# Expert units of one large expert or of four small ones, with all expert weights in one ring

## The chip, the cores and the metric

The kernel runs on one core of a Trainium2 chip. The metric is the device time of one execution in microseconds (us), the median of several. The kernel is one program: an inference step of a hybrid diffusion trunk of one layer, in 32-bit floating point throughout. The change concerns its last part, the mixture of experts.

## The reference, cut to what matters

384 tokens (128 of context, 256 latent) of width 1024 pass adaLN, three mixers and a mixture of 64 SwiGLU experts (width 256), of which each token takes 8:

```python
def moe(x, lp):                        # x: (384, 1024)
    s = sigmoid(x @ lp['w_router']); sel = s + lp['b_router']
    # the 4 best of 8 groups by their two best scores, then the 8 best experts in them
    w = take(s, eidx); w = w / sum(w) * 2.5
    hg = einsum('nd,edf->nef', x, w_gate)          # w_gate, w_up: (64, 1024, 256)
    hu = einsum('nd,edf->nef', x, w_up)
    hid = silu(hg) * hu * combine[:, :, None]
    y = einsum('nef,efd->nd', hid, w_down)         # w_down: (64, 256, 1024)
    return y + shared_expert(x)
```

Gate and up of an expert are 2.097 MB, its down matrix 1.049 MB, together 3.146 MB. How many tokens each expert gets is data. With the drawn inputs the router of the reference puts the 3072 token-expert pairs on 51 of the 64 experts. Sorted, the counts are 139, 129, 125, 124, 124, 118, 118, 116, 112, 112, 111, 110, 107, 107, 105, 103, 100, 96, 95, 87, 83, 78, 74, 70, 67 (25 experts over 64 tokens), 63, 61, 59, 48, 46, 44 (6 from 33 to 64), and 21, 21, 18, 14, 12, 11, 10, 6, 5, 4, 4, 4, 2, 2, 2, 1, 1, 1, 1, 1 (20 up to 32).

## The kernel before, in words

The core's engines each run their own program and meet at semaphores. TensorE (PE) multiplies, VectorE (DVE) and ScalarE (ACT) take its results out of PSUM, SyncE (SP) starts the weight loads, GpSimd (POOL) starts the gathers and scatters of token rows.

The routed experts are worked off in units of 128 token slots. A unit is wide or narrow. A wide unit is one expert with over 64 tokens (two units if it has over 128), a narrow one is two experts of up to 64 tokens, one in slots 0 to 63, the other in 64 to 127. Units run in a fixed rhythm of three places: wide, wide, narrow. DVE works the table of units out of the counts (stage "counts"), TensorE turns it into a row of expert numbers (stage "row") and into the table of slots (stage "table"). With the counts above there are 27 wide and 13 narrow units, 40 in all, numbered 0 to 39.

For each unit DVE makes one-hot rows (`one_hots`), TensorE multiplies them with the table (`index`), DVE takes the indices (`take_index`), POOL gathers the unit's token rows from DRAM (`gather`, only rows in use move, 4 KB each), TensorE transposes them (`transposes`, L2042) and ACT copies them out (`take_xt`). Then, in TensorE's `step(i, p)`:

- transposes of unit i+1
- `gate_up` of unit i, first half of the contraction (a wide unit: L2056, 128 columns; a narrow one: L2058 and L2059, 64 columns each, each with its own expert's weights)
- `hidden_t` of unit i-1 (L2097), `index` of unit i+4 (L1702)
- `gate_up`, second half, which ends with an increment of `gu_ready`
- `down` of unit i-1, which ends with an increment of `dn_ready`: a narrow unit in full precision (L2081, L2082), a wide one in three products of a high and a low part in the faster rounded format (L2071 to L2073). For these ACT makes the high part of the down matrix (`down_high`, L1002) in the one buffer DNH, so it waits until the previous wide unit's down is done, and DVE the low part (`down_low`, L1606).

DVE weights the result (L1630) and POOL scatters it to `y_parts` in DRAM (L1093); the last two units stay in SBUF. At the end SP loads `y_parts` back (L692) in twelve parts of 1 MB, and they are summed, added and normed.

A matmul of two 32-bit operands leaves two records in the profile, one for each of its passes.

The weights have four slots (`WSLOT`) of one expert each: one for either wide place and two for the narrow one. SP works through its list in order. It starts the loads of the first three slots at once, the fourth after the shared expert's last matmuls (`shd_ready`), since that slot holds the shared weights until then. After that the gate/up load of unit i+3 waits for `gu_ready` of unit i, the down load of unit i+2 for `dn_ready` of unit i-1. Each load is one transfer of a whole matrix:

```python
def gate_up_of(r, q):
    e = number(r)
    flat = lambda a: a[bass.ds(e, 1)].rearrange("o p n -> p (o n)")
    sp.dma_start(WSLOT[q][:, 0:2 * KD * DE], flat(w_gu)).then_inc(gu_loaded[q], 16)
```

Of the kernel before, what the change touches and what calls it, by code (L numbers as in the profile page):

```python
# [43 lines left out]
HALF = P // 2  # L44
BIG0 = NE
RTAB = P
RPAD = RTAB + 8
UNITS_MAX = NE // 2 * 3
BODY = 12
PASSES = UNITS_MAX // BODY  # L50
BR_EARLY = 7
HO_BANK = (6, 4, 5)
SH_BANK = (4, 5, 0)
WS, XGS, AHEAD, GAHEAD = 4, 3, 4, 3
# [5 lines left out]
K_ID, K_SEL, K_MASK, K_LEV, K_SCAN, K_TRI, K_ONE, K_R128, K_TOK, K_COL, K_T8, K_END, K_SUB = range(13)  # L60
K_W = [P, 2 * P, GRID_W, 7 * P, T, P, P, P, NT * 4, 2, NG * NG, 0, RTAB]
K_AT = [sum(K_W[:i]) for i in range(14)]

# [5 lines left out]
def shape_constants():  # L69
    k = np.zeros((P, K_AT[13]), np.float32)  # L70
# [19 lines left out]
    put(K_COL, np.stack([r, np.where(r < BIG0, r // 2 * 3 + 3, (r - BIG0) // 2 * 3 + r % 2 + 1)], 1))  # L90
    put(K_SUB, np.tile(np.where(r < BIG0, r % 2 * HALF - 1, -1 - P * (r - BIG0))[None].astype(np.float32), (P, 1)))
# [135 lines left out]
def trunk(nc, x, consts, cols, b_gate, w_ada, w_in, w_br, w_out, rpb, cache_k, cache_v, state, w_router, b_router,  # L227
# [5 lines left out]
    with ExitStack() as ctx:  # L233
# [106 lines left out]
        WSLOT = [bigB[:, 0:6144], bigA[:, 6144:12288], bigA[:, 0:6144], bigB[:, 13824:19968]]  # L340
        GU_W = [w[:, 0:4096].rearrange("p (g k n) -> p g k n", g=2, k=KD) for w in WSLOT]
        DN_W = [w[:, 4096:6144].rearrange("p (k n) -> p k n", k=2) for w in WSLOT]
# [3 lines left out]
        XG = [bigB[:, 19968:20992], bigB[:, 20992:22016], nT_flat[:, 0:D]]  # L346
        HID = cut(bigB, 8192, (2, DE))
# [4 lines left out]
        DNL = [cut(bigB_r, 4096, (2, D)), cut(bigA_r, 10240, (2, D))]  # L352
# [13 lines left out]
        CNT, BIG, END, STA, EON, TMP = (bigD[:, 2112 + 64 * i:2176 + 64 * i] for i in range(6))  # L366
        NSM, NBG, STS, STB, RC = (bigD[:, 1536 + 64 * i:1600 + 64 * i] for i in range(5))
        RK = cut(bigD, 1856, (NT, NE))
# [8 lines left out]
        SUBC = bigD[:, 4280:4280 + RTAB]  # L377
        RHS = cut(bigD_r, 4408, (2, 2, NT, 4))
# [5 lines left out]
        YG = ([cut(bigA, i, (2, D)) for i in (0, 2048, 6144, 8192)]  # L384
              + [cut(bigB, i, (2, D)) for i in (0, 2048, 6144, 13824, 15872, 19968)]
              + [cut(nT_flat, D, (2, D)), cut(bigD, 0, (2, D))])
# [8 lines left out]
        loaded = [sem(f"weights_loaded_{i}") for i in range(NSLOT)]  # L395
        in_small = sem("constants_loaded")
        in_cols = sem("small_vectors_loaded")
        in_x = sem("x_loaded")
        in_cache = sem("cache_then_shared_down_loaded")
        in_state = sem("state_loaded")  # L400
        in_bias = [sem("bias_loaded_then_results_written_0"), sem("bias_loaded_then_results_written_1")]
        bias_masked = sem("bias_masked")
        in_xh = sem("residual_loaded")
# [19 lines left out]
        ada_back = sem("late_ada_loaded")  # L423
# [50 lines left out]
        sh_loaded = sem("shared_weights_loaded")  # L474
        bg_loaded = sem("gate_bias_loaded")
# [31 lines left out]
        gu_loaded = [sem(f"gate_up_loaded_{i}") for i in range(WS)]  # L507
        dn_loaded = [sem(f"down_loaded_{i}") for i in range(WS)]
# [75 lines left out]


        @block.sync
        def _(sp):
# [3 lines left out]
            for n in ISSUE:  # L591
# [20 lines left out]
                elif src == "out":  # L612
                    if i == 0:
# [5 lines left out]
                        sp.dma_start(SUBC, consts[:, K_AT[K_SUB]:K_AT[K_SUB] + RTAB]).then_inc(fin_loaded, 16)  # L619
# [30 lines left out]
            def gate_up_of(r, q):  # L650
                e = number(r)
                flat = lambda a: a[bass.ds(e, 1)].rearrange("o p n -> p (o n)")
                sp.dma_start(WSLOT[q][:, 0:2 * KD * DE], flat(w_gu)).then_inc(gu_loaded[q], 16)

            def down_of(r, q):
                e = number(r)
                sp.dma_start(WSLOT[q][:, 2 * KD * DE:], wd[bass.ds(e, 1)].rearrange("o p n -> p (o n)")).then_inc(dn_loaded[q], 16)
# [6 lines left out]
            for r, q in ((BIG0, 0), (BIG0 + 1, 1), (1, 3)):  # L664
                gate_up_of(r, q)
                down_of(r, q)
# [1537 lines left out]
```

## Time and profile before

| | before |
|---|---|
| median of 3 runs | 1097.4 us (1096.2 to 1100.99) |
| the profiled execution's own time | 1096.59 us |
| its span, first to last instruction | 1094.8 us |
| TensorE busy | 1043.3 us, 95% of the span |
| mean granted TensorE clock | 0.991 of full speed |
| expert loop, first gate/up to the last one's end | 581.91 to 1038.96 us |

A row of the profile names a line of the kernel, the engine, the operation and the tiles it writes and reads. "x" is a count, "idle" the time in which the engine waited before it, with what ended that wait. A DMA share of 1.00 means that the 16 DMA engines always had packets. GB/s is what they moved.

### The profile page before, as it was taken

The numbers are of one execution on the slowest core, as the hardware profiler recorded it, in microseconds if no ns is written. First come the engines' busy times: TensorE is split into PE (matmuls) and PEld (weight loads), VectorE is DVE, ScalarE is ACT, GpSimd is POOL, SyncE is SP. The second block draws the span as 40 slices with busy tenths as digits, with TensorE's granted clock in tenths as the row PEclk, the third lists the DMA queues.
The fourth block names the chain that finished last, engine by engine and source line by source line (L and its number), as shares of the span: only waits on it lengthen the run. The fifth ranks groups of instructions, "written<-read, shape, count | busy, mean of one in ns | idle before, by whom it ended". The sixth has DMA issues, their size and how long they took to land.

```text
span 1094.8 us, 15005 instructions
## 1 busy us (share of the span) xinstructions
PE 1043.3 (95%) x4876; PEld 699.7 (64%) x4876; DVE 533.0 (49%) x1118; ACT 357.3 (33%) x481; POOL 157.0 (14%) x136
## 2 busy tenths in 40 slices
PE   4999999999899999999989999999999999999975
PEld 2599988789788897874645455555555555454532
DVE  1523544445798956945634334433344334333357
ACT  3334444327444445501423222223223222222201
POOL 0020321000000000000010323322322213221000
PEclk9999999999999999999999999999999999999998
DMA  9999775447544323740297999999999999999592
GB/s 387 413 265 395 103 98 92 156 154 258 206 173 154 151 82 98 250 151 1 97 372 272 379 407 397 421 408 396 418 419 424 401 406 421 417 410 411 224 411 104
DMA packets 54912, 306.61 MB, mean 280 GB/s; under 512 B 12550, under 2 KB 16902, under 8 KB 35920
## 3 DMA queue, kind: packets, MB, share of 16 engines
q1 hardware_dynamic: 35280, 270.63, 61.3%
q0 software_dynamic: 12256, 26.80, 10.5%
q10 hardware_dynamic: 7328, 8.55, 2.3%
q8 instruction: 29, 0.48, 0.2%
q14 instruction: 19, 0.16, 0.0%
HBM read 285.31 MB, written 36.85 MB: 294 GB/s over the span
## 4 chain that ended last, share of the span: by engine, by line
PE 58%; DMA 2%; DVE 2%; ACT 1%; issue 1%; DVEq 0%; SPq 0%
PE PS L2056 16%; PE PS L2058 8%; PE PS L2081 4%; PE PS L1945 4%; PE PS L2042 3%; PE PS L1693 3%; PE PS L2071 2%; DMA bigA<-in_w_down 2%; PE PS L2073 2%; PE PS L2072 2%; PE PS L2013 2%; PE PS L2130 1%; PE PS L1935 1%; PE PS L1933 1%; PE PS L1934 1%; PE PS L2097 1%
## 5 line engine op out<-in xcount | busy, mean ns | idle before, releaser
L1093 POOL DMA_INDIRECT y_parts<-bigB,IDX x38 | 73.9, 1944 | 327.2 <-DVE bigB L1630 318.1
L2056 PE MATMUL PS<-bigB 128*128 128x512 f32 x224 | 101.7, 597 | 0.0
L1747 PE MATMUL PS<-bigB_r 128*128 128x384 f32 x288 | 98.5, 342 | 1.3 <-ACT bigB L779 1.3
L1749 PE MATMUL PS<-bigB_r,bigA_r 128*128 128x384 f32 x288 | 96.5, 335 | 0.0
L1748 PE MATMUL PS<-nT_r,bigB_r 128*128 128x384 f32 x288 | 96.3, 334 | 0.0
L1630 DVE TENSOR_SCALAR bigB<-PS,bigD 128x1024 f32<-128x1024 f32 x40 | 51.3, 1283 | 90.2 <-PE PS L2073 55.5
L2058 PE MATMUL PS<-bigA,bigB 128*64 128x512 f32 x208 | 94.8, 598 | 0.5 <-issue 0.5
L2059 PE MATMUL PS<-bigB 128*64 128x512 f32 x208 | 94.8, 598 | 0.0
L2056 PE MATMUL PS<-bigA,bigB 128*128 128x512 f32 x208 | 94.6, 598 | 0.0
L1238 DVE TENSOR_TENSOR bigA_r<-bigA,bigB_r 128x2048 fp32r<-128x2048 f32 x18 | 41.3, 2293 | 97.6 <-ACT bigB_r L805 97.6
L1596 DVE TENSOR_TENSOR bigB<-bigB,PS 128x256 f32<-128x256 f32 x40 | 16.9, 421 | 138.1 <-ACT bigB L989 138.0
L779 ACT ACTIVATE bigB<-PS 128x384 f32<-128x384 f32 (+1 forms) x55 | 27.3, 497 | 141.5 <-PE PS L1749 70.1
L2056 PEld LDWEIGHTS PS<-bigB 128*128 128x128 f32 x224 | 40.6, 190 | 40.7 <-issue 40.7
L1761 PE MATMUL PS<-bigC_r,bigA_r 128*128 128x384 f32 x192 | 65.5, 341 | 0.0
L985 ACT ACTIVATE bigB<-PS 128x1024 f32<-128x1024 f32 x40 | 40.7, 1017 | 66.2 <-PE PS L2042 66.2
L2056 PEld LDWEIGHTS PS<-bigA,bigB 128*128 128x128 f32 x208 | 37.5, 191 | 37.3 <-issue 37.3
L989 ACT ACTIVATE bigB<-PS 128x256 f32<-128x256 f32 x40 | 15.4, 384 | 138.0 <-PE PS L2056 95.8
L1747 PEld LDWEIGHTS PS<-bigB_r 128*128 128x128 f32 x288 | 54.0, 188 | 7.6 <-issue 4.5
L2058 PEld LDWEIGHTS PS<-bigA,bigB 128*64 128x64 f32 x208 | 26.3, 136 | 46.5 <-issue 45.0
L1748 PEld LDWEIGHTS PS<-nT_r,bigB_r 128*128 128x128 f32 x288 | 54.1, 188 | 0.0
L1749 PEld LDWEIGHTS PS<-bigB_r,bigA_r 128*128 128x128 f32 x288 | 54.0, 188 | 0.0
L2071 PE MATMUL PS<-bigC_r,bigB_r 128*128 128x512 f32 x108 | 49.6, 459 | 4.1 <-DVE bigB_r L1611 4.1
(370 smaller groups left out, 2117.9 us busy)
## 6 DMA issues: line engine op xcount, KB each, us to landing
bigB<-in_w_gu SPq DMA_DIRECT2D x27, 2048.0 KB, 17.6
bigA<-in_w_gu SPq DMA_DIRECT2D x26, 2048.0 KB, 15.1
bigA<-in_w_in SPq DMA_DIRECT2D x17, 2048.0 KB, 10.0
bigB<-in_w_down SPq DMA_DIRECT2D x27, 1024.0 KB, 17.9
bigA<-in_w_down SPq DMA_DIRECT2D x26, 1024.0 KB, 18.0
bigA<-in_w_ada SPq DMA_DIRECT2D x8, 2048.0 KB, 9.0
y_parts<-bigB SPq DMA_DIRECT2D x6, 2048.0 KB, 30.1
bigB<-in_w_ada SPq DMA_DIRECT2D x3, 2048.0 KB, 20.2
```

What stands on the lines that cost most here:

```text
L1093: pool.indirect_dma_start(y_parts, bass.IndirectOffsetOnAxis(ap=IDX[:, p, 1:2], axis=0), YS[:, p % 2, :], None, bounds_check=T * TOPK - 1, ...
L1630: nc.vector.tensor_scalar(YS[:, p % 2, :].rearrange("p (a n) -> p a n", a=2), PS[:, 6:8, :], WC[:, p:p + 1], None, ALU.mult).then_inc(ys_d ...
L1747: mm(out, wh, nh, start=(k == 0), stop=False)
L1748: mm(out, wh, nl, start=False, stop=False)
L1749: last = mm(out, wl, nh, start=False, stop=(k == KD - 1))
L1761: last = mm(out, low[:, k, :], NHI2[:, k, :], start=False, stop=(k == KD - 1))
L1945: last = mm(PS[:, 6 + hf, :], G[:, k, m * P:(m + 1) * P], w[:, k, :], start=(k == 0), stop=(k == KD - 1))
L2056: last = mm(PS[:, 2 + b, :], XT[:, b, k, :], GU_W[s][:, :, k, :], start=first, stop=stop)
L2058: mm(PS[0:HALF, 2 + b, :], XT[:, b, k, 0:HALF], GU_W[2][:, :, k, :], start=first, stop=stop)
L2059: last = mm(PS[HALF:P, 2 + b, :], XT[:, b, k, HALF:P], GU_W[3][:, :, k, :], start=first, stop=stop)
L2071: mm(out, HTH[:, b, k, :], DNH[:, k, cols], start=(k == 0), stop=False)
L2081: mm(PS[0:HALF, 6 + hf, :], HT[:, b, k, 0:HALF], DN_W[2][:, k, cols], start=(k == 0), stop=(k == 1))
```

## The change

A unit is now one expert with over 32 tokens (wide), or four experts of up to 32, each in its own 32 slots and its own 32 columns of the matmul. The rhythm has six places: five wide, then one of four. With the counts above that is 33 wide units and 5 of four; the last wide one takes number 38, so there are 39 units, and place 35, the sixth one for a four, is empty: its gate/up and down are left out, its hidden transposes and index product are not.

The weights pass through one ring of 27 places of 512 KB, in the order in which TensorE uses them. A wide expert takes four places for gate/up (two contraction steps in each) and two for down. A unit of four takes sixteen places for gate/up and eight for down: a slice of each of its experts, one transfer per slice, so that it may start when the first slices are there. A rhythm of six uses 54 places, twice round the ring. `w_gu` is laid out anew on the host so that a slice is 4 KB in a row of each partition. TensorE signals after each pair of contraction steps of a four (`quad_used`), so that its places are filled again early. Semaphores of earlier stages are used again for the loads, with a base count. The table of units has other formulas and gains a diagonal matrix (DIAG), a matmul in stage "row" and three in stage "table"; a small load of constants (SUBC) goes. At the end the order of the parts changes: seven of the twelve part loads go to memory that is free by then, the other five wait for the last down.

The diff, cut to its core:

```diff
+PERIOD, BIGS = 6, 5
+RING = 27
...
+def ring_places():
+    at, n = {}, 0
+    order = []
+    for c in range(BIGS):
+        order += [("gu", c, 4), ("dn", c - 1, 2) if c else ("qdn", 0, 8)]
+    order += [("qgu", 0, 16), ("dn", BIGS - 1, 2)]
...
SyncE, start:
+            e = number(0)
+            big_gate_up(e, 0, GU_TO[0])
             sp.wait_ge(n2_out, 48)
...
+            f = number(1)
+            big_gate_up(f, 1, GU_TO[1])
+            big_down(e, 0)
+            e = number(2)
+            big_gate_up(e, 2, GU_TO[2])
+            big_down(f, 1)
+            sp.wait_ge(te_ready, 1)
+            f = number(3)
+            big_gate_up(f, 3, GU_TO[3][0:2])
+            sp.wait_ge(gu_ready, 1)
+            big_gate_up(f, 3, GU_TO[3][2:])
+            big_down(e, 2)
             sp.wait_ge(shd_ready, NT)
+            e = number(4)
+            big_gate_up(e, 4, GU_TO[4])
+            big_down(f, 3)
...
SyncE, one rhythm of six:
+                    e = number(big(0))
+                    with exists(0):
+                        sp.wait_ge(gu_ready, done + 5)
+                        big_gate_up(e, 0, GU_TO[0])
+                    with sp.If(per + 1 <= quads):
+                        experts = quad_numbers(per * -4 + (RTAB - 4))
+                        sp.wait_ge(dn_ready, done + 4)
+                        quad_down(experts, 0)
+                        sp.wait_ge(quad_used, per * 3 + 1)
+                        quad_down(experts, 1)
+                    f = number(big(1))
+                    with exists(1):
+                        sp.wait_ge(quad_used, per * 3 + 2)
+                        big_gate_up(f, 1, GU_TO[1])
+                    with exists(0):
+                        sp.wait_ge(quad_used, per * 3 + 3)
+                        big_down(e, 0)
...
+                    with sp.If(per + 2 <= quads):
+                        experts = quad_numbers(per * -4 + (RTAB - 8))
+                        sp.wait_ge(gu_ready, done + 8)
+                        quad_slices(experts, 0)
+                        sp.wait_ge(dn_ready, done + 7)
+                        quad_slices(experts, 1)
+                        sp.wait_ge(gu_ready, done + 9)
+                        quad_slices(experts, 2)
+                        sp.wait_ge(gu_ready, done + 10)
+                        quad_slices(experts, 3)
+                    with exists(4):
+                        sp.wait_ge(gu_ready, done + 10)
+                        big_down(e, 4)
...
+                    if 4 * m + c == YG_FREE:
+                        sp.wait_ge(dn_ready, units)
TensorE, gate_up:
+                    if k % 2 == 0:
+                        pe.wait_ge(quad_loaded[k // 2], ...)
+                    for h in range(4):
+                        rows = slice(h * FEW, (h + 1) * FEW)
+                        last = mm(PS[rows, 2 + b, :], XT[:, b, k, rows], PIECE[RING_AT["qgu", 0][4 * (k // 2) + h]][:, half],
+                                  start=first, stop=stop)
+                    if k in (1, 3, 5):
+                        last.then_inc(quad_used, 1)
TensorE, down of a four:
+                    for k in range(2):
+                        pe.wait_ge(quad_loaded[4 + k], ...)
+                        for hf in range(2):
+                            for h in range(4):
+                                last = mm(PS[rows, 6 + hf, :], HT[:, b, k, rows],
+                                          PIECE[RING_AT["qdn", 0][4 * k + h]][:, hf * 512:(hf + 1) * 512], ...)
TensorE, stages row and table:
+                    mm(PS[0:1, 1, 2 * RTAB:3 * RTAB], RC[:, 1:2], ident, start=True, stop=True).then_inc(pr_ready, 1)
...
+                        mm(PS[:, 3, m * P:(m + 1) * P], ones, DIAG, start=False, stop=True)
```

## Rows read from the trace of the kernel before

**Rows 1.** The page: DMA busy tenths in 40 slices of the span

```profile
DMA  9999775447544323740297999999999999999592
```

**Rows 2.** The chain that ended last: start, us, what (loop's start and end)

```profile
588.88 0.89 PE PS L2042 x8
...
599.99 0.89 PE PS L2042 x8
...
611.66 0.89 PE PS L2042 x8
612.55 3.44 PE PS L2056 x8
616.44 3.54 PE PS L2056 x8
619.99 0.57 PE PS L2081
...
623.57 1.09 PE PS L2042 x8
...
634.87 0.89 PE PS L2042 x8
...
1038.96 0.57 PE PS L2081
```

**Rows 3.** Stretches: us, busy of each engine, granted clock, DMA share, GB/s

```profile
10.00:30.00 20.00, 15.88 (x92) 8.20 (x96) 5.43 (x20) 7.59 (x16) 0.00 (x0) 1.00 1.02 433
397.40:401.40 4.00, 4.00 (x25) 4.00 (x24) 1.47 (x4) 3.93 (x4) 0.00 (x0) 1.00 1.02 417
549.00:610.00 61.00, 55.64 (x209) 29.81 (x210) 23.63 (x57) 15.84 (x22) 10.87 (x8) 1.00 0.84 333
610.00:1019.00 409.00, 408.31 (x1666) 214.05 (x1665) 154.04 (x339) 104.58 (x128) 107.03 (x69) 1.00 1.00 410
669.60:704.50 34.90, 34.90 (x145) 18.25 (x144) 13.29 (x29) 9.01 (x11) 9.82 (x6) 1.00 0.99 402
809.10:844.00 34.90, 34.90 (x144) 18.24 (x144) 13.29 (x29) 9.01 (x11) 9.81 (x6) 1.00 1.01 421
```

**Rows 4.** DMA issues: tiles, count, KB each, median us to landing

```profile
bigB<-in_w_gu SPq DMA_DIRECT2D x27, 2048.0 KB, 17.6
bigA<-in_w_gu SPq DMA_DIRECT2D x26, 2048.0 KB, 15.1
...
out_y<-bigB SPq DMA_DIRECT2D x3, 512.0 KB, 2.6
```

**Rows 5.** The down loads' line (L657), 600 to 670 us

```profile
DMA to landing us min/median/max: 8.4/13.2/16.0
```

**Rows 6.** The same line, 950 to 1010 us

```profile
DMA to landing us min/median/max: 22.9/24.2/27.1
```

**Rows 7.** Timeline, 32-column matmuls of the conditioning vector's projection

```profile
37.40 1.92 PE L1731 MATMUL PS<-bigD,csil 128*32 128x512 f32 x16
37.86 0.13 PEld L1731 LDWEIGHTS PS<-bigD,csil 128*32 128x32 f32 x4 [0.30 <-issue]
```

**Rows 8.** Timeline, a narrow unit's gate/up

```profile
601.28 0.59 PE L2058 MATMUL PS<-bigA,bigB 128*64 128x512 f32 x1
601.29 0.59 PE L2059 MATMUL PS<-bigB 128*64 128x512 f32 x1
```

**Rows 9.** Timeline of SyncE's queue at the start of the loop

```profile
548.68 0.37 SPq L653 DMA_DIRECT2D bigB<-in_w_gu  x1
...
577.88 0.34 SPq L653 DMA_DIRECT2D bigA<-in_w_gu  x1
...
589.63 0.33 SPq L653 DMA_DIRECT2D bigB<-in_w_gu  x1
```

**Rows 10.** Groups of instructions in the loop: busy us, mean ns, idle before

```profile
L1606 DVE TENSOR_TENSOR bigA_r<-bigA,bigC_r 128x2048 fp32r<-128x2048 f32 x13 | 29.8, 2293 | 10.4 <-ACT bigC_r L1002 9.8
L1002 ACT ACTIVATE bigC_r<-bigB 128x2048 fp32r<-128x2048 f32 x14 | 26.7, 1910 | 9.3 <-DMA bigB<-in_w_down 8.6 <-issue 0.7
```

More of the change, by code:

```diff
@@ L57, with is_big, big_number @@
 PT_BANK = (4, 6, 7)
-K_ID, K_SEL, K_MASK, K_LEV, K_SCAN, K_TRI, K_ONE, K_R128, K_TOK, K_COL, K_T8, K_END, K_SUB = range(13)
-K_W = [P, 2 * P, GRID_W, 7 * P, T, P, P, P, NT * 4, 2, NG * NG, 0, RTAB]
-K_AT = [sum(K_W[:i]) for i in range(14)]
+K_ID, K_SEL, K_MASK, K_LEV, K_SCAN, K_TRI, K_ONE, K_R128, K_TOK, K_COL, K_T8, K_END = range(12)
+K_W = [P, 2 * P, GRID_W, 7 * P, T, P, P, P, NT * 4, 8, NG * NG, 0]
+K_AT = [sum(K_W[:i]) for i in range(13)]
+def is_big(u):
+    return u % PERIOD < BIGS
+def big_number(u):
+    return u // PERIOD * BIGS + u % PERIOD
+def ring_places():
[4 more added lines that the diff above has]
+    order += [("qgu", 0, 16), ("dn", BIGS - 1, 2)]
+    for kind, c, size in order:
+        at[kind, c] = [(n + i) % RING for i in range(size)]
+        n += size
+    assert n == 2 * RING
+    return at
+RING_AT = ring_places()
 C_N1, C_N2, C_C, C_ADA, C_LB, C_CONV, C_HG = range(7)
@@ L506, in trunk @@
         sh_added = sem("shared_added")
-        gu_loaded = [sem(f"gate_up_loaded_{i}") for i in range(WS)]
-        dn_loaded = [sem(f"down_loaded_{i}") for i in range(WS)]
+        gu_loaded = [sem(f"gate_up_loaded_{c}") for c in range(BIGS)]
+        gu_base = (0,) * BIGS
+        dn_loaded = [sem("down_loaded_0"), in_xh, ada_back, in_x, sh_loaded]
+        dn_base = (0, 16, 48, 32, 32)
+        quad_loaded = [in_small, in_cols, in_state, bg_loaded, loaded[0], loaded[1]]
+        quad_base = (16, 16, 32, 16) + tuple(16 * sum(n % NSLOT == i for n, (kind, _) in enumerate(STREAM) if kind in ("in", "ada", "br", "out"))
+                                             for i in range(2))
+        quad_used = sem("quad_slices_used")
+        place_ready = sem("place_offsets")
         oh_done = sem("one_hots")
@@ L674, in _, with matrix @@
[L674 to L685 removed]
+            def matrix(a, e):
+                return a[bass.ds(e, 1)].rearrange("o p n -> p (o n)")
@@ new lines, in big_gate_up, with big_down, quad_numbers, quad_slices @@
+            def big_gate_up(e, c, runs):
+                for to, first in runs:
+                    size = to.shape[-1]
+                    sp.dma_start(to, matrix(w_gu, e)[:, first * D:first * D + size]).then_inc(gu_loaded[c], 16)
+            def big_down(e, c):
+                sp.dma_start(DN_TO[c][0][0], matrix(wd, e)).then_inc(dn_loaded[c], 16)
+            def quad_numbers(first):
+                return [number(first + h) for h in range(4)]
+            def quad_slices(experts, j, hs=range(4)):
+                for h in hs:
+                    sp.dma_start(PIECE[RING_AT["qgu", 0][4 * j + h]],
+                                 matrix(w_gu, experts[h])[:, j * D:(j + 1) * D]).then_inc(quad_loaded[j], 16)
```

345 lines of the change are left out of this document (199 added, 146 removed).

## The prediction

> **What bounds the kernel now.** I read the page's head first, then the stretches, then the chain that ended last through the expert loop, then the loads. TensorE is busy 95% of the span and the ending chain is mostly its own, but from the 23rd slice on the DMA engines are full too [rows 1]. So two things must be asked of the expert loop: which of them sets its pace, and how far behind the other is.
>
> The chain through one round of the loop (wide, wide, narrow) is TensorE without a gap: 599.99 to 634.87, 34.88 us, and steps of 11.67, 11.91 and 11.30 us [rows 2]. The step between two wide units is 11.11 us at the start (588.88 to 599.99) and 11.30 later [rows 2]; I take 11.2, and so a narrow unit costs 34.88 - 3 x 11.2 = 1.3 us more than a wide one. Inside a step: transposes 0.9, the gate/up matmuls 3.44 + 3.54, 0.45 between for the hidden transposes and the index, and the down matmuls 2.8 for a wide unit (what is left of 11.30), 3.6 (619.99 to 623.57) for a narrow one [rows 2].
>
> The stretches say how near DMA is. From 610 to 1019 its share is 1.00 at 410 GB/s [rows 3]. The need of a round is four experts of 3.146 MB [rows 4] and about 230 token rows of 4 KB read and written, 14.5 MB in 34.88 us, 415 GB/s. So DMA is not merely busy: it falls behind. A down load takes a median of 13.2 us to land between 600 and 670, and 24.2 us between 950 and 1010 [rows 5, 6], and ScalarE already waits for such loads, 8.6 us in one group [rows 10]. TensorE sets the pace now with nothing left behind it.
>
> **The change: TensorE's work.** The router's counts give 27 wide units and 13 narrow ones before, 33 wide and 5 of four after, numbers 0 to 38, number 35 an empty place. Is a 32-column matmul as quick four at a time? The projection of the conditioning vector already does it: 16 records of 128*32 by 512 take 1.92 us together, the weights of each four 0.43 us after those of the four before [rows 7]; the 64-column ones run in twos, 0.01 us apart [rows 8], and the 8 twos of a narrow down take 3.6 us [rows 2], the same 0.43 to 0.45 each. So a unit of four takes a narrow unit's time: 16 slots for gate/up, 8 for down. Bounds: no dearer than a narrow unit (1.3 over a wide one), and, if four went only as two and two, 7.2 + 3.6 us more.
>
> From the end of unit 0's gate/up (588.88) to the last gate/up's end (1038.96) is 450.1 us [rows 2]. One unit fewer is -11.2; eight narrow ones fewer -10.4; the empty one saves its matmuls (7.0 + 2.8) but uncovers its neighbour's split of the down matrix, ScalarE 1.91 and VectorE 2.29 [rows 10] and hops, 4.5 us, less 1.4 of transposes and index: -6.7 (minus 9.8 plus 3.1). The table gains three matmuls and the row one, at 0.11 us a record (eight of that size in 0.89 [rows 2]): +0.8 before unit 0. Together -27.5 us: TensorE alone would give 1097.4 - 28 = 1070.
>
> **The change: the loads.** The bytes do not fall. 33 + 20 = 53 loads of an expert, as many as the 27 + 26 of before [rows 4]; the token rows are the same 3072 pairs. What changes is when they are wanted. Six units now need nine experts, 28.3 MB, and some 473 rows (five wide units of 89 on the mean, 28 for a four) both ways, 3.9 MB: 32.2 MB in 6 x 11.2 + 1.3 = 68.5 us, 470 GB/s. The fastest stretch of the trace is 433 [rows 3]. At 410 the six take 78.5 us. The last eight wide units want only 3.9 MB in 11.2 us and cannot give the time back, since TensorE sets their pace. Finer slices bring no rate: the branch weights, in 4 KB rows, ran at 417 GB/s (397.4 to 401.4), the loop's mixture at 410 [rows 3]. I use 410; the 35 us stretches of the loop go from 402 to 421 [rows 3], and these are the bounds.
>
> The start costs too. Before, six loads go out from 548.68, a pair at 577.88, the next at 589.63 [rows 9]; DMA is partly idle until 610. After, 19 places (9.96 MB) can go at once, with 316 gathered rows 11.3 MB, 27.5 us from 549.0. Then SyncE waits for unit 0's gate/up, for one place, and behind it in the queue stand the loads of units 2 to 4, free at 577.9 but not issued. It resumes at 590.4 (589.63 plus the 0.8): idle 13.9 us. Before, the share of 0.84 to 610 leaves 61 x 0.16 = 9.8 us idle [rows 3].
>
> **The sum.** (1) Landing of unit 28's down matrix, issued behind the fifth four's gate/up slices: 262 places are 137.4 MB, the gathers to unit 30 and scatters to unit 28 19.0 MB; 549.0 + 13.9 + 156.4/0.410 + 1.3 for landing (512 KB alone land in 2.6 us, half of it transfer [rows 4]) = 945.7. (2) Splitting it 4.5, its down 2.8, unit 30's transposes and gate/up 8.4, the four's down 3.6, transposes 0.9: TensorE is ready for unit 31 at 965.9. (3) Unit 31's weights are place 278: 165.6 MB in all, landed at 968.1; its gate/up (7.4) ends 975.5. (4) Then TensorE sets the pace: three steps to 1009.1; down of 33 and the uncovered split around the empty place, down of 34: 1019.2; gates of 36 and 37 without a down between, to 1035.9; a down and the last gate/up, 1046.1. That is 7.1 us after 1038.96.
>
> Behind it the tail is as before: before, a narrow down of 3.6 and the last split stand between the last gate/up and the last down; after, a wide down of 2.8 and the split, which waits for it; and the part rows, 12.6 MB, start at the last gate/up's end. Five of the twelve part loads now wait for the last down, 2.8 + 4.5 + 2.8 = 10 us, under the 17.9 that the first seven (7.34 MB) take: nothing. More index work for a four (8 small instructions of VectorE for 4) lies in its idle time: it is busy 13.29 of 34.9 us [rows 3]. So 1096.6 + 7.1 = 1103.7; the profiled execution is 0.8 us under the median shown: 1104.
>
> The same sum at 402 GB/s starts unit 31 at 975.6 instead of 968.1: 1112. At 421 it starts at 958.2: 1094.
>
> The Trainium skill, "DMA: Bandwidth & Descriptors", section "Where 436 GB/s comes from", puts the ceiling of the SBUF ports at 435 GB/s and the HBM side of one core at about 358, and says that the latter binds a load from HBM. The 358 does not hold here: 410 over 409 us [rows 3]. By the 435 the need of 470 is beyond reach as well, and the time would come out near that of the second rival.
>
> **Rivals.**
> *More gaps between loads (slower).* One queue in order of use: slices of a four wait for dn_ready and quad_used counts, and wide loads behind them wait though their places are free. For: 12 us of such waiting at the start alone. Against: a round's loads are released by events one to four units ahead, and the landing delay of 13 to 24 us keeps engines fed. Price: each idle microsecond in the first five sixes is one of time; 2 to 3 in each, 10 to 15: 1114 to 1119.
> *The rate rises (faster).* All loads move at the start's 433. Unit 31 then starts at 948: 1084.5. It decides above about 424 GB/s. Against: the loop has gathers and scatters throughout, and never shows over 421.
> *TensorE alone sets the end (faster).* 1070; needs 470 GB/s.
> *Fours run as two and two.* 5 x 10.8 = 54 us on 1070: 1124; the loads then hide. Against: the fours of [rows 7].
> *Nothing happens within error.* It is the forecast's own mechanism at 411 to 424.
>
> **How the numbers follow.** A measurement tells 0.5%, 5.5 us, from no change: under 1092 is faster, over 1103 slower. Chances: forecast 0.62 (own range 1094 to 1112; a little under half of it within 0.5%), gaps 0.18, rate 433 0.10, fours as two and two 0.06, TensorE alone 0.04. Faster: 0.14 and a sliver of the forecast, 0.15. Same: 0.28. Slower: the rest. The range leaves out TensorE alone, the two and two, most of rate 433 and the upper end of the gaps: 1092 to 1116.
>
> **What would show it.** Right: 39 units; the gate/up matmuls of a four start in fours 0.43 us apart; from unit 5 to unit 31 TensorE idle for DMA, mostly at unit 4's down of each six and at the fours' slices, 9 to 10 us in each six; DMA share 1.00 at about 410 from 590 to 1030; a hole in DMA from 576 to 590; wide steps of 11.2 in the last eight. Wrong: a loop rate over 424; steps of 11.2 all through; a four's gate/up of 14 us; DMA holes after 600.

## The result and the profile after

The kernel after takes 1130.3 us (median of 4, 1128.4 to 1130.9), the kernel before 1097.6 on the same chip: ratio 1.029, 95% interval 1.026 to 1.032. 1104 was forecast: the direction is right, the size is not, by 26 us. The profiled execution took 1130.05 us, its span is 1128.2.

The page's DMA slices, its two busiest queues and the chain by line; against [rows 1] the share of the last third is as full, with 375 to 403 GB/s in its weaker slices, and loads stand in the ending chain:

```profile
DMA  9999864357344343621569999999999999967592
GB/s 387 418 265 352 100 95 85 150 210 258 151 150 150 151 150 95 239 74 38 230 248 387 373 420 414 411 416 378 424 403 381 418 397 375 396 277 260 224 390 114
q1 hardware_dynamic: 49248, 270.57, 60.5%
q0 software_dynamic: 11968, 26.35, 10.3%
PE PS L2202 14%; DMA bigA<-in_w_down 6%; PE PS L2088 4%; PE PS L1836 3%; SPq L727 3%; PE PS L2223 2%; PE PS L2188 2%; PE PS L2225 2%; PE PS L2224 2%; DMA bigB<-in_w_down 2%; DMA bigB<-in_w_gu 2%; PE PS L2159 2%; PE PS L2298 2%; SPq L722 1%; DMA nT<-n_rows,IDX 1%
```

What was forecast of the fours is there. The timeline of TensorE shows the first eight-slice gate/up of a four, by place and start; four records lie within 0.02 us, the next four 0.43 later, as in [rows 7]:

```profile
636.71 0.62 PE L2208 MATMUL PS<-bigA,bigB 128*32 128x512 f32 x1
636.72 0.62 PE L2208 MATMUL PS<-nT,bigB 128*32 128x512 f32 x2
636.73 0.62 PE L2208 MATMUL PS<-bigB 128*32 128x512 f32 x1
637.16 0.59 PE L2208 MATMUL PS<-bigA,bigB 128*32 128x512 f32 x1
```

The pace of the sixes is read from the transposes that stand ahead of the gate/up of the first unit of each (units 6, 12, 18, 24, 30). "Unit n's transposes" means this place everywhere here; by the order of a step they turn the rows of unit n+1.

```profile
647.38 1.04 PE L2188 MATMUL PS<-K,bigB 128*128 128x128 f32 x8
732.01 1.05 PE L2188 MATMUL PS<-K,bigB 128*128 128x128 f32 x8
813.23 1.14 PE L2188 MATMUL PS<-K,bigB 128*128 128x128 f32 x8
893.20 1.05 PE L2188 MATMUL PS<-K,bigB 128*128 128x128 f32 x8
974.88 1.04 PE L2188 MATMUL PS<-K,bigB 128*128 128x128 f32 x8
```

The sixes take 84.6, 81.2, 80.0 and 81.7 us, where 78.5 were forecast. TensorE's waits from 600 to 1000 stand where they were expected: at the fourth slices of a four, and at downs. There the low part of the hidden (L1754) stands in VectorE's program behind that of the down matrix, ScalarE's part of that matrix comes before it, and ScalarE waits for the load:

```profile
PE PS L2223 <- DVE bigB_r L1754: 18.6, 7, 4.6
PE PS L2208 <- DMA bigD<-in_w_gu: 16.6, 4, 5.3
PE PS L2202 <- DMA bigB<-in_w_gu: 2.7, 1, 2.7
```

```profile
965.70 1.91 ACT L1141 ACTIVATE bigC_r<-bigB 128x2048 fp32r<-128x2048 f32 x1 [17.06 <-DMA bigB<-in_w_down]
```

The windows (columns as in [rows 3]; the last two are the share of the DMA engines and GB/s) say what is new. From 640 to 980 the rate is 403, not 410, and for 10 to 30 us in each six it dips to between 323 and 380. In the deepest dip the share falls too: engines run dry. The share hides most of it: from 930 to 940 half of the 4 KB load packets still take 159 ns, but the longest is counted as busy for 1.8 us. Behind its waits TensorE is also granted less clock, 0.93 on this stretch where the kernel before has 1.00.

```profile
576.00:592.00 16.00, 13.90 (x52) 7.88 (x53) 5.70 (x10) 3.50 (x5) 2.27 (x2) 1.00 0.34 121
600.00:640.00 40.00, 40.00 (x175) 24.04 (x173) 20.02 (x33) 13.95 (x15) 13.53 (x7) 1.00 1.00 394
640.00:980.00 340.00, 302.60 (x1331) 165.75 (x1328) 119.26 (x243) 79.98 (x96) 73.79 (x52) 0.93 1.00 403
850.00:860.00 10.00, 10.00 (x40) 6.20 (x39) 4.20 (x7) 2.51 (x4) 3.91 (x2) 1.00 0.98 352
930.00:940.00 10.00, 10.00 (x36) 5.90 (x35) 4.13 (x10) 2.51 (x5) 3.91 (x2) 1.00 0.93 323
```

**Where the 26 us arise.** Unit 0's gate/up starts at 584.6 (581.9 before): 2.7, of which the forecast has 0.8, so 1.9 too late. Unit 31's gate/up ends at 995.4, forecast 975.5: 19.9 too late with these 1.9, so 18.0 arise in the stretch that DMA bounds. From the end of unit 34's gate/up (1029.5, forecast 1009.1) to the last gate/up's end (1072.4) are 42.9 us, forecast 37.0: 5.9. The tail behind it is 55.8 as forecast. 1.9 + 18.0 + 0.5 (three steps) + 5.9 = 26.3. At the end, in the timeline and in a window: the token rows of unit 38, the last one, come late to unit 37's transposes, and behind TensorE's wait of 3.5 us the granted clock is 0.79 between 1050 and 1058, in part its lower level, 1.2 of 2.4 GHz:

```profile
1025.81 3.68 PE L2202 MATMUL PS<-bigA,bigB 128*128 128x512 f32 x8
1051.95 1.75 PE L2188 MATMUL PS<-K,nT 128*128 128x128 f32 x8 [3.49 <-DMA nT<-n_rows,IDX]
1068.73 3.68 PE L2202 MATMUL PS<-bigB 128*128 128x512 f32 x8
```

```profile
1050.00:1058.00 8.00, 6.05 (x16) 3.50 (x17) 3.48 (x4) 2.18 (x2) 2.75 (x1) 0.79 0.91 381
```

The trace also keeps the 16 increments that each load gives its semaphore, one when each DMA engine is done. These are two loads of a wide unit's down matrix, in us behind their issue, the times sorted:

```
before, issued 647.4     12.8 12.9 13.0 13.5 13.5 13.5 13.7 13.8 14.7 15.0 15.0 15.6 15.6 16.0 16.0 16.0
after, issued 882.8     11.9 12.3 12.5 12.5 12.7 12.8 12.8 13.4 13.4 14.4 14.7 15.8 17.5 21.4 24.2 26.2
```

The load counts as landed at the last. This lag of the last behind the middle one (the ninth), as a mean over the down loads of a stretch, grows in both kernels: before 1.7 us (640 to 680), 8.5 (880 to 920), 11.8 (1000 to 1040); after 3.2 (640 to 680), 13.2 (880 to 920), 10.7 (960 to 1000). Before, TensorE never waited for it: its waits from 600 to 1000 are 0.7 us in all.

### The profile page after: what moved, and what is told of

It is laid out like the page before. It is cut to its first block, busy times and chain, and to the rows that moved or that the text cites. A ratio compares the mean times of both kernels' runs of the same rounds, so it can differ in the third digit from the quotient of the medians.

```text
span 1128.2 us, 15199 instructions
## 1 busy us (share of the span) xinstructions
PE 1033.6 (92%) x4895; PEld 711.8 (63%) x4895; DVE 546.0 (48%) x1110; ACT 364.8 (32%) x484; POOL 158.3 (14%) x134
## 4 chain that ended last, share of the span: by engine, by line
PE 43%; DMA 11%; SPq 5%; issue 2%; DVE 2%; ACT 2%; POOLq 0%; DVEq 0%; ACTq 0%; POOL 0%
PE PS L2202 14%; DMA bigA<-in_w_down 6%; PE PS L2088 4%; PE PS L1836 3%; SPq L727 3%; PE PS L2223 2%; PE PS L2188 2%; PE PS L2225 2%; PE PS L2224 2%; DMA bigB<-in_w_down 2%; DMA bigB<-in_w_gu 2%; PE PS L2159 2%; PE PS L2298 2%; SPq L722 1%; DMA nT<-n_rows,IDX 1%
## 5 line engine op out<-in xcount | busy, mean ns | idle before, releaser
L2202 PE MATMUL PS<-bigB 128*128 128x512 f32 x272 | 127.7, 609 | 2.7 <-DMA bigB<-in_w_gu 2.7
L2202 PE MATMUL PS<-bigA,bigB 128*128 128x512 f32 x232 | 105.7, 597 | 0.0
L2223 PE MATMUL PS<-bigC_r,bigB_r 128*128 128x512 f32 x132 | 66.1, 501 | 25.3 <-DVE bigB_r L1754 25.3
L2202 PEld LDWEIGHTS PS<-bigB 128*128 128x128 f32 x272 | 50.3, 195 | 53.3 <-issue 50.4
L2202 PEld LDWEIGHTS PS<-bigA,bigB 128*128 128x128 f32 x232 | 42.2, 191 | 43.5 <-issue 43.5
L1141 ACT ACTIVATE bigC_r<-bigA 128x2048 fp32r<-128x2048 f32 x20 | 38.2, 1911 | 66.6 <-DMA bigA<-in_w_down 35.2
L2208 PE MATMUL PS<-bigB 128*32 128x512 f32 x200 | 43.8, 705 | 16.6 <-DMA bigD<-in_w_gu 16.6
L1749 DVE TENSOR_TENSOR bigB_r<-bigB,bigC_r 128x2048 fp32r<-128x2048 f32 x13 | 29.8, 2292 | 57.0 <-ACT bigC_r L1141 56.5
L2223 PEld LDWEIGHTS PS<-bigC_r,bigB_r 128*128 128x128 f32 x132 | 27.0, 205 | 46.0 <-DVE bigB_r L1754 35.1
L1749 DVE TENSOR_TENSOR bigA_r<-bigA,bigC_r 128x2048 fp32r<-128x2048 f32 x20 | 45.8, 2291 | 20.5 <-ACT bigC_r L1141 19.7
L2224 PE MATMUL PS<-bigC_r,bigB_r 128*128 128x512 f32 x132 | 54.9, 416 | 0.0
```

What stands on the lines that cost most here:

```text
L1749: nc.vector.tensor_tensor(DNL[p % PERIOD], DN_W[p % PERIOD], DNH.bitcast(F32), ALU.subtract).then_inc(dn_low, 1)
L2202: last = mm(PS[:, 2 + b, :], XT[:, b, k, :], PIECE[RING_AT["gu", c][k // 2]][:, half], start=first, stop=stop)
L2208: last = mm(PS[rows, 2 + b, :], XT[:, b, k, rows], PIECE[RING_AT["qgu", 0][4 * (k // 2) + h]][:, half], start=first, stop=stop)
L2223: mm(out, HTH[:, b, k, :], DNH[:, k, cols], start=(k == 0), stop=False)
L2224: mm(out, HTL[:, b, k, :], DNH[:, k, cols], start=False, stop=False)
```

## The experiments

Each is an edit of the kernel after unless it says "before". The single profile of each differs in where the loop starts (unit 1's transposes at 590.7 to 595.9 in those of the kernel after and its variants), so gains in the loop are read from unit times and the whole from medians. The runs were measured at different times; the kernel before had medians of 1096.7 to 1098.2 beside them, so a difference of a microsecond or two between two runs says nothing.

**1. Is it DMA's volume at all?** Fours' loads cut.

```
-  sp.dma_start(PIECE[r], matrix(w_gu, experts[h])[:, j*D:(j+1)*D])
+  n = D // 4 if r not in (7, 8, 16, 17, 22, 23) else D
+  sp.dma_start(PIECE[r][:, 0:n], matrix(w_gu, experts[h])[:, j*D:j*D+n])
```

> 18 of the 24 places of a four get only the first quarter of their columns, from the second four's gate/up and the first four's down on (places into which ScalarE's or VectorE's halves of a down matrix are written keep their whole load); waits, number and order of transfers stay, and the products of the fours are not the reference's. About 31 MB of some 190 are left out. Theory A (DMA's volume holds the kernel after back): TensorE alone sets the loop: 1070 by the prediction's sum, + 2.7 for the later first gate/up, + 5 to 9 for the late gather of unit 37: 1073 to 1084. Theory B (the waits in the one queue hold it back, whatever the bytes): over 1105.

Measured 1077.2 us (1076.1 to 1078.0), ratio 0.979. The waits of TensorE from 600 to 1000, all of them:

```profile
PE PS L2228 <- DVE bigB_r L1759: 2.3, 1, 2.3
PE PS L1850 <- DVE bigD_r L1280: 1.0, 1, 1.0
PE PS L2193 <- DMA nT<-n_rows,IDX: 0.6, 1, 0.6
```

This is theory A. With the bytes gone a six takes 68.1 us, where 68.5 were summed, but the whole is 1077, not 1070: DMA costs 53 us over that, where 34 were forecast. From the end of unit 34's gate/up to that of the last one this run takes 41.0 us where 37.0 were forecast. The down of unit 34, behind the uncovered split (the wait of 2.3 us above), takes 5.3 us and not 2.8: the granted clock is 0.50, its lower level of 1.2 GHz:

```profile
984.10:989.40 5.30, 5.25 (x12) 4.01 (x13) 0.39 (x3) 0.00 (x0) 1.43 (x2) 0.50 0.92 359
```

**2. The hole at the start.** `wait_ge(gu_ready, 1)` and the three loads behind it that need unit 0's places moved behind those that need none.

```
 big_gate_up(f, 3, GU_TO[3][0:2])
-sp.wait_ge(gu_ready, 1)
-big_gate_up(f, 3, GU_TO[3][2:]); big_down(e, 2)
 sp.wait_ge(shd_ready, NT)
+big_gate_up(g, 4, GU_TO[4][1:]); big_down(f, 3); quad_slices(experts, 0, range(3))
+sp.wait_ge(gu_ready, 1)
+big_gate_up(f, 3, GU_TO[3][2:]); big_down(e, 2); big_gate_up(g, 4, GU_TO[4][0:1])
```

> Loads whose places are free at about 578 (unit 4's gate/up but its first place, unit 3's down, three slices of the first four: 4.2 MB, 10 us at 410 GB/s) go out ahead of SyncE's wait for unit 0's gate/up. Theory A (bytes against time up to unit 31): the hole of 576 to 591 shrinks by 8 to 10 us and the end comes 7 to 10 earlier: 1120 to 1123. Theory B (waits inside the loop set the pace, or the order of use): less than 3 earlier: 1127 or more.

Measured 1130.1 (1129.8 to 1130.4): no gain. Theory A missed. The windows show why:

```profile
576.00:592.00 16.00, 13.59 (x49) 7.58 (x50) 5.90 (x10) 3.54 (x6) 2.29 (x2) 1.00 0.85 320
600.00:640.00 40.00, 40.00 (x172) 24.29 (x174) 19.74 (x33) 14.00 (x15) 13.25 (x7) 1.00 0.85 294
```

The hole is filled (0.85 for 0.34) and comes back from 600 to 640 (0.85 for 1.00): with the ring full, the next load waits for a place. From 549 to 660 both have moved the same 38.1 MB.

**3. Rows of 8 KB for the fours**, three of four gate/up slices and all downs in pairs of neighbouring places:

```
-  dma_start(PIECE[4*j+h], matrix(w_gu, experts[h])[:, j*D:(j+1)*D])         # two of these
+  dma_start(joined([QGU[j][h], QGU[j+1][h]]), matrix(w_gu, experts[h])[:, j*D:(j+2)*D])
```

> The fours' loads take pairs of places with rows of 8 KB: a gate/up is 3 transfers of 1 MB and 2 of 512 KB for two slices in place of 8, a down 4 of 1 MB in place of 8. Theory A (a packet of 4 KB took 168 ns in the kernel after, 8 KB 315, 16 KB 623, so 4 KB rows move 5% slower): the rate between 600 and 980 rises from 402 to about 408 GB/s and the end comes 4 to 8 us earlier, 1122 to 1126. Theory B (rows of 4 KB cost nothing, the coarser transfers land later): 1129 to 1134.

Measured 1130.4 (1126.6 to 1132.3). The rate from 640 to 980 rose to 408, three sixes (units 12 to 30) took 241.0 us for 242.9, and the step from unit 30's to 32's transposes gave 1.6 of it back. Both are under what the medians of the whole can tell: neither theory is decided by them.

**4. The price of a short row, in the kernel before.** Its loads cut by columns.

```
+for j in range(4): sp.dma_start(WSLOT[q][:, j*D:(j+1)*D], flat(w_gu)[:, j*D:(j+1)*D])
```

> The kernel before, with each gate/up load cut into 4 transfers and each down load into 2, all of 4 KB rows; schedule and waits as they were. Theory A (4 KB rows are 5% dearer, and the kernel before stands at DMA's limit, 415 GB/s wanted of 411): at 392 a round takes 37.0 us instead of 34.9, less some 10 us that the loads run ahead: 1107 to 1122. Theory B (slices cost nothing; the kernel after lost its rate elsewhere): 1095 to 1101.

Measured 1111.4 (1109.7 to 1113.1), ratio 1.011 (1.006 to 1.016): theory A. The same bytes, waits and instructions of TensorE become 13 us slower at 397 GB/s instead of 411, with the engines full. From 640 to 980 a load packet of 4 KB takes 165 ns on the mean, where the kernel before has 8 KB in 312 and 16 KB in 635.

```profile
640.00:980.00 340.00, 330.93 (x1354) 173.66 (x1352) 121.79 (x270) 82.29 (x103) 74.01 (x57) 1.00 1.01 397
```

**5. Was it the number of transfers?** The same count, cut by partitions (`WSLOT[q][32*j:32*j+32, ...]` for a gate/up, 64 for a down).

> The kernel before with as many transfers as in the run with 4 KB rows (4 for a gate/up, 2 for a down), but cut by partitions, so that rows stay 16 and 8 KB long. Theory A (the length of a row was the price of 13 us there): 1095 to 1101. Theory B (the number of transfers was, on SyncE or at the queue): 1107 to 1114.

Measured 1435.1 (1423.5 to 1438.1), ratio 1.305: outside both theories, so nothing is said on the count of transfers: whether run 4 paid for the short rows or for the many transfers stays open. The cut itself is ruinous, with the engines full:

```profile
640.00:980.00 340.00, 220.46 (x784) 109.91 (x782) 73.32 (x163) 47.61 (x60) 34.32 (x34) 0.84 1.02 235
```

Packets of 16 KB took 1126 ns for 635.

**6. The gather behind the empty place.**

```
 with exists(1):
-    sp.wait_ge(quad_used, per * 3 + 2)
-    big_gate_up(f, 1, GU_TO[1])
+    with sp.If(per + 1 <= quads): sp.wait_ge(quad_used, per * 3 + 2); big_gate_up(f, 1, GU_TO[1])
+    with sp.Else(): big_gate_up(f, 1, GU_TO[1])
```

and so for the next two loads.

> In a round without a four, SyncE issues the loads of units 1 and 2 of the next round (and unit 0's down) without waiting for the empty place; their places are free long before. They go out at about 1029.7 instead of 1034.6 to 1037.3, so that the gather of unit 37's rows (issued 1037.8, landed 14.1 us later) finds a shorter queue. Theory A (that late gather, and the lower clock behind it, cost 5 to 9 us): 1121 to 1126. Theory B (the loads only move up, the gather stands behind as much): 1128 to 1132.

Measured 1131.4 (1126.8 to 1134.1): theory B. (The gather that the expectation gives to unit 37 is that of unit 38's rows.) The time from unit 35's to unit 36's transposes got longer by as much as that from unit 36's to 37's got shorter (from unit 35's to 37's transposes 19.95 us, 19.85 in the kernel after, 19.57 with the fours cut). The late gather is not what the end costs.

**7. No token rows.** `bounds_check=0` for gather and scatter.

> The gathers and scatters keep their instructions but the bounds let only index 0 through: nearly all of the 24 MB of token rows is left out, and the output is not the reference's. The loads alone still want 28.3 MB in 68.5 us, 413 GB/s, so DMA stays full. In the kernel after, the last of the 16 increments of a wide down's load comes 3.2 us behind the middle one at 640 to 680, 8.8 at 800 to 840 and 13.2 at 880 to 920. Theory A (the valid rows stand in the first partitions and load some of the 16 engines more than the others): this lag stays under 4 us, and the end is at 1078 to 1092. Theory B (one engine is slow by itself, or the loads are uneven): the lag grows to over 8 us and the end is at 1090 to 1105.

Measured 1076.0 (1075.9 to 1076.9). Theory A on the lag; on the time better than both, TensorE alone again, though the loads by themselves fill the engines at 411 GB/s from 640 to 960:

```profile
640.00:960.00 320.00, 319.24 (x1492) 176.97 (x1491) 135.37 (x272) 90.72 (x107) 83.48 (x56) 1.00 1.02 411
```

```
issued 901.8            13.2 13.2 13.4 13.4 13.7 13.9 14.2 14.3 14.5 14.5 14.6 14.8 14.9 14.9 15.2 15.6
```

The lag of the last behind the middle stays at 0.6 to 1.4 us on the mean up to 1000. So the token rows make the engines uneven, not the loads. It also tests the order of the loads: every load and every wait of SyncE is as in the kernel after, and TensorE waits 3.7 us in all from 600 to 1000.

**8. All three edits of 2, 3 and 6.**

> The kernel after with the start filled, 8 KB rows for the fours, and the loads behind the empty place issued early. From the runs so far the first gives nothing, the second at most 3 us, the third 5 to 9 by theory A of its own run: 1118 to 1126. If the DMA volume up to unit 31 alone sets the end, and the end's gather is one of its consequences: 1127 to 1131.

Measured 1129.4 (1127.8 to 1130.8): the second reading. The end's gather is a consequence of what happens up to unit 31.

**9 to 11. Other partitions for the same rows.** Which row of a unit goes to which partition is set by the constant that the one-hots are compared with.

```
-slots = kc(K_R128)                                        # partition p takes row p
+slots = kc(K_R128).rearrange("p (a b) -> p b a", b=16)    # (p mod 8)*16 + p div 8
```

> The one-hots of a wide unit put its rows into the partitions in another order: partition p takes row (p mod 8) x 16 + p div 8, so that the valid rows (89 of 128 on the mean) stand in every group of 8 partitions, not in the first ones; the same rows move. Theory A (the engines share a row transfer by groups of neighbouring partitions, and the first ones are late for it): the last increment of a wide down's load comes under 4 us behind the middle one, where it was 13 at 880 to 920, TensorE waits 6 to 11 us less up to unit 31, and the end is at 1119 to 1125. Theory B (the engines take partitions in turn, p mod 16, and the lag is from elsewhere): now rows leave out whole engines, the lag grows beyond 20 us and the end is at 1135 or more. Theory C (the lag goes, but the mean rate of DMA is what binds): 1127 to 1131.

Measured 1127.8 (1126.6 to 1131.8). The time is theory C's, but the lag did not go, so none of the three fits: it fell from 13.2 to 8.3 at 880 to 920, and from unit 6's to unit 37's transposes the run took 403.7 us, the kernel after 404.6.

> The order of rows as in the run before, with the start filled, 8 KB rows for the fours and the early loads behind the empty place. Theory A: the lag's 6 to 11 us and up to 4 for the rate of the 8 KB rows, which could not show while the slowest engine bound: 1114 to 1122. Theory C: 1125 to 1130. Both leave it slower than the kernel before.

Measured 1129.6 (1126.8 to 1131.8): in theory C's range, and no better than without the other three edits.

> The same order of rows in the kernel before, wide and narrow units. Its loads lag too (last behind middle: 1.7 us at 640 to 680, 8.5 at 880 to 920, 11.8 at 1000 to 1040), but none makes TensorE wait. Theory A: the lag stays under 4 us, the time within 0.5%: 1093 to 1100. Theory B: the lag doubles and TensorE begins to wait: 1103 or more.

Measured 1095.5 (1094.7 to 1098.3), ratio 0.999 (0.997 to 1.000): no change, as theory A has it. The lag fell, to 2 to 6 us from 860 on where it was 6 to 12, and the increments now stand in two lots of eight:

```
before, issued 914.8     9.6  9.9 10.4 10.4 10.6 10.7 10.7 10.7 11.0 11.0 11.1 11.7 11.7 13.4 13.8 20.3
this run, issued 915.2   9.2  9.2  9.3  9.3  9.4  9.5  9.5  9.6 13.6 13.8 13.9 14.3 15.1 15.2 15.5 16.5
```

This order fills every group of 8 neighbouring partitions alike, so engines that shared rows by such groups would not split into eight early and eight late ones. The rule of run 17 gives just that: a unit's first 64 rows all go to the eight engines with even numbers.

**12, 13. Rotation by 40 partitions a unit**, in a second instruction of VectorE.

```
+s = 40 * (u % BODY) % P        # partitions s.. take rows 0.., partitions ..s the last rows
+for lo, hi, r in ((s, P, 0), (0, s, P - s)): tensor_tensor(OH[:, b, :, lo:hi], kc(K_R128)[:, r:r+hi-lo], ...)
```

> A wide unit's rows keep their order but start 40 partitions further in each unit, so that over a six every group of partitions, however the engines share them, takes a like number of rows. Theory A (TensorE waits for the slowest engine, and uneven rows cost pace): lag of the last increment under 4 us, a six 2 to 3 us shorter than 81, end at 1115 to 1122. Theory C (the engines' mean rate binds, the lag is only latency): the lag falls, a six stays within 1 us of 81, end at 1127 to 1131.

Measured 1134.9 (1132.7 to 1138.7), slower than both theories say, yet unit 37's transposes came at 1038.9 instead of 1051.95. The 13 us gained, and 3 more, are lost behind that point. 10 of these 16 go to VectorE's first instruction behind the loop, which comes late (timeline of this kernel, then of the kernel after; in brackets the idle time ahead of it):

```profile
1091.59 1.27 DVE L1824 TENSOR_SCALAR bigC<-K,small 128x128 f32<-128x128 f32 x6 [14.48 <-issue]
```

```profile
1090.26 1.27 DVE L1817 TENSOR_SCALAR bigC<-K,small 128x128 f32<-128x128 f32 x6 [4.47 <-issue]
```

> The same with the fours' loads in 8 KB rows. Theory A: 1113 to 1120. Theory C: a six 0.6 us shorter as in the earlier runs with 8 KB rows, 1125 to 1130.

Measured 1133.9 (1133.0 to 1135.2), again neither theory's; the same gap, 14.51 us. In it the DMA queue of instructions moves four packets of 8 KB, in run 12 at 1080.4, 1085.4, 1086.7 and 1091.7 (below, its queue from 1076 to 1092); the kernel after has none there, its next one is at 1094.2.

```profile
q14 instruction: 4, 0.03, 0.5%
```

**14. Bytes out of the downs alone** (as in 1, gate/up slices whole).

> 6 of the 8 places of each four's down matrices get only the first quarter of their columns (a half of the products of the fours' downs is not the reference's): 11.8 MB less, all of it before unit 31, number and order of transfers kept. Theory C (bytes over a rate of 400 GB/s set the sixes): 29 us less, 1099 to 1104. Theory D (TensorE waits for the lump of gate/up slices, whatever comes beside it, since the ring holds little more than one four ahead): 10 to 20 us less, 1110 to 1120.

Measured 1112.7 (1110.8 to 1115.7): theory D's number. But the slowest engine gives it too: 25.9 MB of loads in a six over 16 engines, at 4096 B in 160 ns (the mean of a row packet here), are 63.3 us, its 87.6 row packets (438 in five sixes, counted as below) are 14.0: 77.3, and the four sixes took 77.5 on the mean. So this run does not tell theory D from the slowest engine.

**15, 16. The shift without a longer program.** Blocks of 32 partitions turned in cycles of four units by another view: none, `[:, ::-1, :]` of halves, of quarters, and `[:, :, ::-1]` of halves.

> The rows of a wide unit are shifted against the partitions by blocks of 32 in turn (none, halves swapped, four blocks reversed, each half reversed), by another view of the constant in the same instruction, so that VectorE's program keeps its length; the run that rotated with a second instruction had unit 37 begin 13 us earlier and lost 16 us after the loop, where VectorE stood 14.5 us ahead of its first instruction behind it, 4.5 before. Theory A (the slowest engine sets the sixes; VectorE's longer program was the loss): unit 37's transposes 8 to 13 us earlier than 1052, VectorE's gap back at 4.5, end at 1117 to 1123. Theory E (an earlier end of the loop is lost in the tail anyway): 1128 or more.

Measured 1118.8 (1117.5 to 1120.6), ratio 1.020 (1.018 to 1.022): theory A; VectorE's gap is 4.47 again. The lag is 7.6 at 880 to 920, down from 13.2, and the dips went, 415 GB/s with a share of 1.02 from 640 to 980:

```profile
647.44 1.04 PE L2197 MATMUL PS<-K,bigB 128*128 128x128 f32 x8
964.37 1.04 PE L2197 MATMUL PS<-K,bigB 128*128 128x128 f32 x8
```

```profile
640.00:980.00 340.00, 305.49 (x1385) 169.18 (x1382) 121.90 (x248) 81.50 (x98) 74.95 (x53) 0.96 1.02 415
```

> The same with the filled start, the 8 KB rows and the early loads behind the empty place. Theory A: some 2 to 6 us more, since with the engines even the mean rate binds and the longer rows raise it: 1112 to 1120. Still slower than the kernel before.

Measured 1116.1 (1115.2 to 1118.2): theory A, 2.8 us under run 15.

**17, 18. Consecutive rows on consecutive engines.** Three copies ahead of the loop make, in a constant that is no longer used, the slots `row = 16*j + engine` for wide units, and the like within each 32 of a four.

> Theory A sharpened. The Trainium skill, DMA: Bandwidth & Descriptors, section The descriptor swizzle, says that engine 8 x (p div 64) + (p div 4) mod 8 serves partition p. With the router's counts and valid rows in the first partitions, the busiest engine moves 438 row packets of the loop's first five sixes, the mean one 284; in the spread order 422, rotated by 40 it moves 340, turned by blocks 362. At 160 ns a packet the busiest is 24.6, 22.0, 8.9 and 12.4 us over the mean, so against the kernel after the spread order should give 2.6, the rotation 15.7 and the turn 12.2 us; they gave 2.5, 13 (up to unit 37) and 11.5. Here consecutive rows go to consecutive engines by that rule, fours too: busiest 312, 4.4 us over the mean. Theory A with that rule: 20 us less than the kernel after, 1108 to 1113. If the rule is only roughly right: 1114 to 1119. If the rule does not hold here: 1120 or more.

Measured 1114.7 (1110.3 to 1117.3), ratio 1.016 (1.013 to 1.019). The median is in the range of "only roughly right"; the profiled run (1110.3) is in that of the rule itself, with unit 37's transposes 18 us earlier and the wide downs' lag under 3 us everywhere.

```profile
646.69 1.04 PE L2196 MATMUL PS<-K,bigB 128*128 128x128 f32 x8
958.11 1.05 PE L2196 MATMUL PS<-K,bigB 128*128 128x128 f32 x8
```

```profile
640.00:980.00 340.00, 311.15 (x1399) 172.41 (x1399) 125.59 (x259) 83.64 (x101) 74.78 (x54) 0.96 1.02 415
```

> The same with the filled start, 8 KB rows and the early loads behind the empty place, which gave 2.8 us on top of the turn: 1105 to 1111, still above the kernel before (the need of a six, 470 GB/s, stays above what DMA moves).

Measured 1110.9 (1108.7 to 1111.7), ratio 1.011 (1.008 to 1.014): the best of this scheme, still slower than the kernel before, as expected. No version beat it.

## Why the prediction was right in direction and wrong in size

**TensorE's work.** Fours in one time slot: right [rows 7]. The wide step of 11.1 to 11.2 and the six of 68.5: right (68.1 and 68.4 in runs 1 and 7). "TensorE alone would give 1070" was 7 us too low: 1077 in two unlike runs (1, 7). 4.0 of the 7 are around the empty place, where 37.0 us were summed and 41.0 measured; 2.5 of these are one down at the lower clock level, which the sum had at full clock. The rest is mostly the later first gate/up.

**The need.** 32.2 MB a six, which DMA cannot move in TensorE's time: right. Without the rows, or without most of the fours' bytes, the loss is gone.

**The step that failed: "At 410 the six take 78.5".** They took 81.9 on the mean. The step took the mean rate of the 16 engines from a trace in which no one waited for the slowest. Where TensorE waits for a load, it waits for its last engine. Valid rows stand in the first partitions, so by the mapping of run 17 the busiest engine moves 438 row packets in five sixes and the mean one 284, 24.6 us more at 160 ns. The others run ahead first (the first of the four sixes took 84.6 us at a full 415 GB/s) and then dry, which is the dip to 323 in the windows. The gains against the kernel after, as that count gives them, from unit 6's to unit 37's transposes, and of the median:

```
order of rows   busiest engine's packets   gain by the count   units 6 to 37   median
spread                    422                     2.6               0.9          2.6
rotated                   340                    15.7              13.2         -4.6 (VectorE's gap)
turned                    362                    12.2              11.6         11.5
even                      312                    20.2              17.3         15.7
```

The count also gives the length of a six: 69.1 us of loads on each engine and the busiest one's rows make 83.1, 82.6, 80.0, 80.7 and 79.1 us for the kernel after, spread, rotated, turned and even; 81.9, 81.7, 78.8, 79.2 and 77.9 were measured, in the same order. So the even run reaches the 78.5 forecast, and its unit 31's transposes come 16.8 us before the kernel after's, 0.7 of them from the start: 16.1 of the 18.0 that the stretch had cost too much. The mapping is the Trainium skill's, DMA: Bandwidth & Descriptors, section The descriptor swizzle, and the runs agree with it. The same page, section iDMA fabric — 4 AXI ports for 8 engines, asymmetric across TPBs, says beside another measurement that a bulk load runs at the pace of its slowest engine; the lag of the last increment, 13.2 us at 880 to 920, is this kernel's case of it.

**"Finer slices bring no rate"** was right as said, and hid a loss: they cost rate. Cutting all loads into slices of 4 KB rows costs the kernel before 13 us (4), by the rows' length or by the number of transfers (5 does not tell). In the kernel after the slowest engine covers this: 8 KB rows with two more edits gave 0.9 us (8) and none with the spread rows (10), and 2.8 and 3.8 once the rows were more even (16, 18).

**The hole at the start** was seen rightly and priced wrongly: its 13.9 us are in the sum, and filling it gave 0 (2), because the ring's 27 places bound how far loads run ahead. This error made the forecast up to 13.9 us later, and so nearer to the result: that is luck.

**The end.** 5.9 us too little: 4.0 of them are TensorE's own (1). The tail of 55.8 and the five part loads at no cost: right.

**Rivals.** "More gaps between loads" named a size near the measured one (2 to 3 us in each six, where 3.4 came; 1114 to 1119 in all, where 1130 came) and the wrong cause: the gaps are engines that have nothing left while one is late, not SyncE's order. With the same order and the same waits but without the rows there was no loss (7), and loads that were moved ahead at the start and at the end changed nothing (2, 6). Rate 433, two and two, and TensorE alone did not come.

**Open.** Why unit 0 starts 0 to 5 us later from profile to profile. And what the lower clock behind the waits costs in the sixes: from unit 6's to unit 30's transposes TensorE is busy for 290.1 us in the kernel after, 282.7 in the even run and 272.4 with the fours' loads cut, for the same work. Whether this lengthens the sixes, or is hidden in the wait for the next load, no run shows.

## What to carry to other kernels

Before a change raises the need on DMA, don't price it by the mean share and rate: look at how far the last of a load's 16 increments lies behind the middle one, and whether some traffic (partly filled gathers and scatters) always uses the same partitions. A hole in the loads' stream is worth only what the buffers behind it can still take in. And 32 MB in 68 us was beyond reach with even engines too: a change that shortens TensorE's work where DMA is full must take bytes out, not move them.

## What the hardware showed unexpectedly

- Loads of 32 or 64 partitions ran at 235 GB/s with all engines full (5). The Trainium skill, SBUF — State Buffer, section Door 1: The DMA port swizzle, says that only half of the 16 ports lie under a range of 32 or 64 partitions and gives about 218 GB/s for it; the run, with loads of full width for its token rows among them, is near it.
- The landing of a load says nothing on the other 15 engines: in the load shown they were done 12 to 16 us after issue on most, and 26.2 on the last.
- VectorE's first instruction behind the loop came 14.5 us after its last one in the loop, in place of 4.5, in the two kernels with one more instruction for most units (12, 13), while the part rows filled DMA (422 GB/s from 1072 to 1085). Four packets of 8 KB on the queue of instructions fall into that gap, none into the gap of the kernel after. So the program was being fetched there; that VectorE waited for it is the likely reading, the trace does not name the engine.
- SyncE's issue of a load takes 0.33 us on the median with up to seven loads outstanding, and 0.7, 1.4 and 2.0 us with eight, nine and ten, at most 7.2 (kernel after, 540 to 1060). The kernel before never has more than six outstanding from 600 to 1000, and no issue there takes over 0.34 us.
